# Chunked scan in a hybrid diffusion layer: step weights folded into the exponent, the mask on GpSimd, the sums' loads from ScalarE

## The reference

```python
dt_f = softplus(dt_f + dt_bias_f); dt_b = softplus(dt_b + dt_bias_b)
def ssd_scan(x, dt, a_log, b_in, c_in, init_state):
    A = -exp(a_log)
    xdt = x * dt[..., None]
    a_cs = cumsum((dt * A).reshape(bsz, nc, CHUNK, h), axis=2)
    seg = a_cs[:, :, :, None, :] - a_cs[:, :, None, :, :]
    decay_in = exp(where(lower, seg, -inf))
    scores = einsum('bclhn,bcshn->bclsh', Ch, Bh)
    y_diag = einsum('bclsh,bcshp->bclhp', scores * decay_in, xdt)
    ...
y_f, s_f = ssd_scan(xs, dt_f, a_log_f, bm, cm, init_f)
y_b, s_b = ssd_scan(fl(xs), fl(dt_b), a_log_b, fl(bm), fl(cm), init_b)
y = y_f + fl(y_b) + d_skip[:, None] * xs
```

## Time and profile before

| | |
|---|---|
| median of 3 runs | 2670.51 us (2668.92 to 2671.6) |
| run of the profiled execution | 2666.11 us, span 2664.4 us |
| TensorE busy | 2464.3 us (92%), weight loads 2169.4 us |
| VectorE / ScalarE / GpSimd busy | 2092.3 (79%) / 1095.0 (41%) / 843.7 us (32%) |
| mean granted TensorE clock | 0.968 |

### The profile page before, as it was taken

The page is one execution under the profiler, slowest core; times in us unless marked ns, Lnnn a source line. Parts: engine busy times, 40 slices in busy tenths (PEclk is TensorE's granted clock), DMA queues, the critical chain, the costliest instruction groups (busy, mean ns, idle before and its releaser), DMA issues.

```text
span 2664.4 us, 38495 instructions
## 1 busy us (share of the span) xinstructions
PE 2464.3 (92%) x14858; PEld 2169.4 (81%) x14858; DVE 2092.3 (79%) x3722; ACT 1095.0 (41%) x1785; POOL 843.7 (32%) x621
## 2 busy tenths in 40 slices
PE   6889999999889977997999887999999999999997
PEld 5778888888777767996886786888888888888886
DVE  3767777726667774543999796999999999999999
ACT  4335656534545544314444582333333333233333
POOL 0000000005667660100343583444334434343431
PEclk9999999999999998998999998999999999999998
DMA  7421121235455445332123489999999999999996
GB/s 305 177 105 70 69 99 69 87 133 170 129 182 156 140 140 174 143 135 103 64 71 106 150 243 381 418 417 418 412 419 416 417 408 415 400 415 417 418 409 249
DMA packets 177671, 642.60 MB, mean 241 GB/s; under 512 B 15600, under 2 KB 84304, under 8 KB 117072
## 3 DMA queue, kind: packets, MB, share of 16 engines
q1 hardware_dynamic: 136016, 361.17, 37.7%
q0 software_dynamic: 36864, 268.45, 24.5%
q10 hardware_dynamic: 4608, 10.52, 1.3%
HBM read 580.23 MB, written 59.72 MB: 240 GB/s over the span
## 4 chain that ended last, share of the span: by engine, by line
PE 71%; DVE 16%; DMA 6%; issue 3%; ACT 3%; SPq 1%; DVEq 0%; POOL 0%; PEldq 0%; PEld 0%; ACTq 0%; POOLq 0%
PE c_pp L885 8%; PE p_pa L2606 5%; PE p_pa L2608 5%; PE p_pa L2607 5%; PE p_py L2625 5%; PE p_py L2623 5%; PE p_py L2624 5%; PE o_ps L1718 4%; PE e_ps L2423 4%; PE s_pg L1418 3%; PE p_py L2637 3%; PE g_ps L1093 2%; DMA w_raw<-in_w_stream 2%; PE a_ps L833 2%; DMA s_sums<-sum_rows 2%
## 5 line engine op out<-in xcount | busy, mean ns | idle before, releaser
L2588 POOL DMA_INDIRECT p_uv<-in_uv_rows,merged x256 | 399.8, 1562 | 616.6 <-DVE merged L2761 555.2
L2606 PE MATMUL p_pa<-h2D,w_hi 128*128 128x384 f32 x896 | 318.8, 356 | 19.9 <-DVE w_lo L2715 19.8
L2761 DVE SCALAR_TENSOR_TENSOR merged<-p_uv,p_sw,merged 128x1024 f32<-128x1024 f32 x256 | 328.6, 1284 | 7.1
L2744 DVE CUSTOM_DVE_ANT_0 p_uv<-p_uv,merged 128x1024 f32<-128x1024 f32 x256 | 307.9, 1219 | 10.8 <-DMA p_uv<-in_uv_rows,merged 10.7
L2608 PE MATMUL p_pa<-h2D,w_lo 128*128 128x384 f32 x896 | 303.0, 338 | 0.0
L2607 PE MATMUL p_pa<-h2D,w_hi 128*128 128x384 f32 x896 | 302.9, 338 | 0.0
L2657 ACT ACTIVATE w_hi<-w_raw 128x2048 fp32r<-128x2048 f32 x110 | 210.3, 1912 | 150.5 <-PE p_py L2625 85.6
L2715 DVE TENSOR_TENSOR w_lo<-w_raw,w_hi 128x2048 fp32r<-128x2048 f32 x110 | 251.7, 2288 | 24.9 <-ACT w_hi L2657 24.9
L2623 PE MATMUL p_py<-w_hi,p_wh 128*128 128x512 f32 x672 | 265.4, 395 | 1.2 <-DVE w_lo L2715 1.2
L2625 PE MATMUL p_py<-w_hi,p_wl 128*128 128x512 f32 x672 | 265.3, 395 | 0.0
L2624 PE MATMUL p_py<-w_lo,p_wh 128*128 128x512 f32 x672 | 265.1, 394 | 0.0
(11 more groups left out here) (403 smaller groups left out, 6018.0 us busy)
## 6 DMA issues: line engine op xcount, KB each, us to landing
w_raw<-in_w_stream SPq DMA_DIRECT2D x174, 1024.0 KB
s_sums<-sum_rows SPq DMA_DIRECT2D x40, 512.0 KB, 6.7
g_pairs<-e_st SPq DMA_DIRECT2D x5, 4096.0 KB, 16.9
p_g<-g_pairs SPq DMA_DIRECT2D x64, 320.0 KB
t_ada<-in_w_ada SPq DMA_DIRECT2D x16, 1024.0 KB, 9.5
xc_dram<-c_xc SPq DMA_DIRECT2D x8, 1284.0 KB, 5.4
p_ve<-in_v_early SPq DMA_DIRECT2D x8, 1024.0 KB, 13.1
r_ur<-in_u_early ACTq DMA_DIRECT2D x14, 512.0 KB, 3.7
```

Source lines behind the costliest of these rows:

```text
L2588: nc.gpsimd.indirect_dma_start(uv[:, k % RING, :], None, K.uv_rows, bass.IndirectOffsetOnAxis(K.sidx[:, t, c:c + 1], 0)).then_inc(K.gather ...
L2606: nc.tensor.matmul(ps_a[m][:, :], wh[:, k, cols], K.h2D[0][:, k, :], start=k == 0, stop=False)
L2744: nc.vector.tensor_tensor_reduce(uv[:, b, 0:D], uv[:, b, 0:D], K.hrow[:, t, :], 1.0, 0.0, ALU.mult, ALU.add, sa[:, at:at + 1]).then_inc(do ...
L2761: nc.vector.scalar_tensor_tensor(ys[:, t, :], uv[:, b, D:2 * D], sw[:, at:at + 1], ys[:, t, :], ALU.mult, ALU.add).then_inc(v_done, 1)
```

## The change

The step size goes into the exponent: step size × exp(sum − own sum) becomes exp(sum + (log of the step size − own sum)). `K.minus_sums` becomes `K.offsets`. Both directions get an exponential of their own, and the half that doesn't belong is set to −1e30 in the spread sums before.

- Tokens: VectorE bounds the step size from below (`s2`), ScalarE takes Ln of it and the exponential of minus that, VectorE makes one correction step of the logarithm from it (two instructions) and subtracts the own sums (two). ScalarE's two copies of `minus_sums` go. TensorE's first transposes wait for the decays and for the offsets.
- GpSimd makes `outside` once (0 or −1e30), and in each step adds it to the loaded sums in place (`mask`), one instruction of 128 × 1024 behind `skip` of the step before; it waits for the load. `weights` goes.
- ScalarE takes eight exponentials of 128 columns with a bias column, the forward ones into `M`, the backward ones into `B`. `shift` goes. They wait for `mask`, for `outputs` and for `mix` of two steps before. Then ScalarE waits for its own exponentials and issues the load of the sums of step b + 2. SyncE loads only those of steps 0 and 1.
- VectorE adds `B` to `M` instead of multiplying by the weights. `lesser` goes.

```diff
@@ -356,7 +356,8 @@
     row = sb("q_row", [P, 2 * UC]); b_row = sb("q_brow", [P, 2 * UC])
-    dtA = sb("q_dtA", [P, NT, 64]); sums_row = sb("q_sums", [P, 4 * P])
+    dtA = sb("q_dtA", [P, NT, 64]); logs = ax; logs_done = sem("t_logs"); inv_done = sem("t_inv"); offsets_done = sem("t_offsets")
+    sums_row = sb("q_sums", [P, 4 * P])
@@ -497,11 +498,13 @@
         S.hi(act, 2, 0)
+        act.wait_ge(dtA_done, 1)
+        nc.scalar.activation(logs[:, :, :], s2[:, :, :], ACT.Ln).then_inc(logs_done, 1)
+        act.wait_ge(logs_done, 1)
+        nc.scalar.activation(ex[:, :, :], logs[:, :, :], ACT.Exp, scale=-1.0).then_inc(inv_done, 1)
         act.wait_ge(cum_mm, 2)
...
             nc.scalar.activation(K.decay[:, 3 * j:3 * j + 3, :], ps_cum[j], ACT.Exp).then_inc(cum_exp, 1)
-        for j in range(2):
-            nc.scalar.activation(K.minus_sums[:, j, :], ps_cum[j][:, 0, :], ACT.Copy, scale=-1.0).then_inc(cum_exp, 1)
         for i in range(PAIRS):
@@ -618,10 +621,17 @@
         link(nc.vector.tensor_scalar(nega[:, :], nega[:, :], -1.0, None, ALU.mult))
+        link(nc.vector.tensor_scalar(s2[:, :, :], K.dt[:, :, :], 1.0e-37, None, ALU.max))
         nc.vector.tensor_tensor(dtA[:, :, :], K.dt[:, :, :], nega[:, :].unsqueeze(1).to_broadcast([P, NT, 64]),
...
         S.lo(dve, 2, 0)
+        dve.wait_ge(inv_done, 1)
+        link(nc.vector.tensor_tensor(ex[:, :, :], ex[:, :, :], s2[:, :, :], ALU.mult))
+        link(nc.vector.scalar_tensor_tensor(logs[:, :, :], ex[:, :, :], -1.0, logs[:, :, :], ALU.add, ALU.add))
         dve.wait_ge(cum_exp, 2)
+        for j in range(2):
+            nc.vector.tensor_tensor(K.offsets[:, j, :].rearrange("p (c h) -> p c h", c=NT), logs[:, :, 32 * j:32 * j + 32],
+                                    ps_cum[j][:, 0, :].rearrange("p (c h) -> p c h", c=NT), ALU.subtract).then_inc(offsets_done, 1)
         for r, d in ((1, 0), (4, 1)):
@@ -675,7 +685,8 @@
             else:
-                pe.wait_ge(cum_exp, 4)
+                pe.wait_ge(cum_exp, 2)
+                pe.wait_ge(offsets_done, 2)
             for j in range(4):
@@ -1155,8 +1166,7 @@
     sums = [sb(f"s_sums{i}", [P, 2, HPG, P]) for i in range(2)]
-    X = sb("s_X", [P, HPG, P])
-    W = [sb(f"s_W{i}", [P, HPG, P]) for i in range(2)]; half_W = sb("s_half_W", [P, HPG, P])
+    outside = sb("s_outside", [P, 2, P]); B = [sb(f"s_B{i}", [P, HPG, P]) for i in range(2)]
     M = [sb(f"s_M{i}", [P, HPG, P]) for i in range(2)]
...
@@ -1211,6 +1221,11 @@
         return a, b, f
+    def load_sums(queue, b):
+        g, c = b // NT, b % NT
+        queue.dma_start(sums[b % 2][:, :, :, :].rearrange("p d h l -> p d (h l)"),
+                        K.sum_rows[c, :, 4 * g * P:(4 * g + HPG) * P].partition_broadcast(P)).then_inc(sums_in[b % 2], 16)
@@ -1233,13 +1248,6 @@
-        def load_sums(b):
...
         def store_states(g):
@@ -1262,7 +1270,7 @@
         for b in range(2):
-            load_sums(b)
+            load_sums(sp, b)
         for s in range(2):
@@ -1273,8 +1281,6 @@
                 store_states(q // NT - 1)
-            if NT <= q < NT + STEPS - 2:
-                load_sums(q - NT + 2)
             if q >= 1:
@@ -1320,20 +1326,16 @@
-        def weights(b):
...
-            nc.gpsimd.tensor_tensor(w, w, half_W[:, :, :], ALU.add).then_inc(W_done, 1)
+        def mask(b):
+            rows = sums[b % 2][:, :, :, :]
+            pool.wait_ge(sums_in[b % 2], 16 * (b // 2 + 1))
+            nc.gpsimd.tensor_tensor(rows, rows, outside[:, :, :].unsqueeze(2).to_broadcast([P, 2, HPG, P]), ALU.add).then_inc(masked, 1)
+        for d, tri in enumerate((K.tri_le, K.tri_ge)):
+            nc.gpsimd.tensor_scalar(outside[:, d, :], tri[:, :], 1.0e30, -1.0e30, ALU.mult, ALU.add).then_inc(outside_done, 1)
+        pool.wait_ge(outside_done, 2)
+        mask(0)
         for q in range(SLOTQ):
@@ -1341,10 +1343,10 @@
                     carry(g, 5)
-            if q >= NT - 1 and q - NT + 1 < STEPS:
-                weights(q - NT + 1)
             if b is not None:
                 skip(b)
+                if b + 1 < STEPS:
+                    mask(b + 1)
         K.clear_previous(pool)
@@ -1463,22 +1465,20 @@
-        def shift(b):
+        def exps(b):
             g, c = b // NT, b % NT
-            act.wait_ge(sums_in[b % 2], 16 * (b // 2 + 1))
-            if b:
-                act.wait_ge(E_done, b)
-            for h in range(HPG):
-                at = c * HEADS + 4 * g + h
-                nc.scalar.activation(X[:, h, :], sums[b % 2][:, 0, h, :], ACT.Identity,
-                                     bias=K.minus_sums[:, 0, at:at + 1]).then_inc(shifted, 1)
-        def exps(b):
-            act.wait_ge(least, HPG * (b + 1))
+            act.wait_ge(masked, b + 1)
             if b >= 2:
                 act.wait_ge(y_mm, b - 1)
-            nc.scalar.activation(M[b % 2][:, :, :], X[:, :, :], ACT.Exp).then_inc(E_done, 1)
+                act.wait_ge(EE_done, b - 1)
+            for d, out in enumerate((M[b % 2], B[b % 2])):
+                for h in range(HPG):
+                    at = c * HEADS + 4 * g + h
+                    nc.scalar.activation(out[:, h, :], sums[b % 2][:, d, h, :], ACT.Exp,
+                                         bias=K.offsets[:, d, at:at + 1]).then_inc(E_done, 1)
+            if b + 2 < STEPS:
+                act.wait_ge(E_done, 2 * HPG * (b + 1))
+                load_sums(act, b + 2)
@@ -1514,8 +1514,6 @@
                 exps(b)
-            if q >= NT - 1 and q - NT + 1 < STEPS:
-                shift(q - NT + 1)
             for u, i in todo[:split_point(todo)]:
@@ -1544,22 +1542,11 @@
-        def lesser(b):
...
         def mix(b):
             m = M[b % 2][:, :, :]
-            dve.wait_ge(E_done, b + 1)
-            dve.wait_ge(W_done, b + 1)
-            nc.vector.tensor_tensor(m, m, W[b % 2][:, :, :], ALU.mult).then_inc(WE_done, 1)
-            dve.wait_ge(WE_done, b + 1)
+            dve.wait_ge(E_done, 2 * HPG * (b + 1))
+            nc.vector.tensor_tensor(m, m, B[b % 2][:, :, :], ALU.add).then_inc(EE_done, 1)
+            dve.wait_ge(EE_done, b + 1)
             dve.wait_ge(sc_mm, b + 1)
@@ -1593,8 +1580,6 @@
                 finish(f)
-            if q >= NT - 1 and q - NT + 1 < STEPS:
-                lesser(q - NT + 1)
             if a is not None:
@@ -2898,7 +2883,7 @@
         K.ssq = sb("ssd_ssq", [P, NT, GROUPS])
-        K.dt, K.minus_sums = sb("dt", [P, NT, 64]), sb("minus_sums", [P, 2, NT * HEADS])
+        K.dt, K.offsets = sb("dt", [P, NT, 64]), sb("offsets", [P, 2, NT * HEADS])
         K.decay = sb("decay", [P, 6, NT * HEADS])
...
             K.hT = [h_ctx.enter_context(nc.sbuf_tensor(f"hT{i}", [P, KD, T], F32R)) for i in range(2)]
```

26 lines of the change are left out of this document (2 added, 24 removed).

## The result

The changed kernel takes 2656.22 us (2652.48 to 2656.86, four runs) where the kernel before, timed again beside it, takes 2671.06 (2668.92 to 2671.71, four runs): a ratio of 0.9943, with a 95% interval of 0.9926 to 0.996. That is 14.8 us faster, where 35 had been forecast. The direction and the range hold; the size is not the forecast's but near that of the second rival (2653).

What follows compares the result with a forecast made beforehand. TensorE was taken to bound the kernel, losing time in the scan to waits on ScalarE and VectorE and a lower clock. −11.4 − 11.6 − 5 − 9 + 2 = −35 us gave 2636 us; 8 in 10 range 2618 to 2662.

Steps and rivals of the forecast that it cites:

- the second rival: GpSimd's mask holds VectorE through `finish`; price 17 us, total 2653 us, chance 0.10.
- VectorE's loop (−11.4): `finish`, `lesser`, `weighted` run before TensorE's next `states`; dropping `lesser` shortens ten waits for `s_xs`, −11.4 us.
- So 0.3 us a step: VectorE's cost when GpSimd's mask meets the third and later instructions of `finish`: 0.3 us a step.
- The mask's own length (2.25 us, bounds to 2.56): GpSimd's mask of 1024 elements takes 2.25 us, bounds 1.28 and 2 × 1.28.
- 2.4 us to spare, so nothing for the wait itself: GpSimd's mask ends at about 708.2 us, ScalarE wants it at 710.6, so the wait costs nothing.
- The end of the scan (−5): From 980 us, TensorE's waits for `s_M` shrink without `lesser` ahead of `mix`: 1.2 us in four slots, −5 us.
- The loads (−11.6): Sums loaded two slots ahead, past SyncE's group loads: TensorE's 14.6 us of waits go, 3 put back, −11.6 us.
- the forecast's five: TensorE's five load-loop waits, four for z pieces and the last for a gate piece, together 14.6 us.
- ScalarE (+2): ScalarE's eight exponentials and load issue mostly fit its cover; +2 us for slots with Silu and a weight split.
- The first rival: ScalarE becomes the late one, its later copies costing TensorE; price some 20 us, total 2656, chance 0.12.
- The clock (−9): Stretches of TensorE's lower clock behind waits go with those waits: −9 us, bounds 0 and −16.
- The token phase (0 or +0.7): Once, extra VectorE instructions and ScalarE's Ln and Exp with one or two table loads: 0 or +0.7 us.

Runs made afterwards that it cites:

- b1: The kernel before without `lesser`, so without the backward half of the exponents; 2648.79 us, ratio 0.9925.
- b2: The kernel before with SyncE issuing the load of sums ahead of everything else of its slot; 2649.98 us, ratio 0.9935.
- e2: The changed kernel with the mask on only 16 of the 128 columns, at the same place; 2624.66 us, ratio 0.9835.
- e3: The changed kernel with the loads of sums issued by SyncE again, at their old place behind the group's loads; 2649.53 us, ratio 0.9926.
- e8: e6 with the loads of sums issued by SyncE behind the group's loads, as in e3; 2646.53 us, ratio 0.9912.
- e6: The changed kernel with the mask whole on VectorE, behind `mix` of the step before; 2666.11 us, ratio 0.9988.
- e9: e8 with VectorE's mask moved ahead of `mix`, nothing left out; 2632.31 us, ratio 0.9864.
- e11: e9 with the loads of sums issued by ScalarE again, as in the changed kernel; 2640.33 us, ratio 0.9894.
- e4: The changed kernel with the mask replaced by two fills of the same elements, which read nothing from SBUF; 2633.23 us, ratio 0.9867.

## Why the prediction was right or wrong

**VectorE's loop (−11.4): failed as forecast, and by one term.** That `lesser` lies on the loop and what it is worth was right: b1 shows −11.7. The step that failed is "So 0.3 us a step" for the meeting of mask and `finish`. It measured 1.4 us a step, and the meetings with the mask alone come to 1.1. Two readings led there. I placed the mask from one slot, in which it would end as the third instruction begins. Over the 27 slots from 700 to 960 us it starts between 1.7 us before and 5.2 after TensorE's outputs begin, with a median of 1.4 after; the third instruction starts 2.16 after, and in 23 of the 27 the mask has not ended by then. And I counted one instruction, while all of VectorE's with two SBUF operands can be met: the additions, the product, the weighted rows and `mix`. The row with 3.09 us had been read the earlier trace rows, and the blocking stood in the rival; the median of 0.427 us spoke for the small price, but it is the median of an instruction that met none of the three weight instructions in the whole scan, so it says nothing of what a meeting costs.

**The mask's own length (2.25 us, bounds to 2.56): right,** 2.34 to 2.41 us in 33 of 40 (2.468 mean).

**Its "2.4 us to spare, so nothing for the wait itself": wrong.** The exponentials wait for it 29.9 us. At the end of the scan the two faults feed each other. GpSimd, then ScalarE, then TensorE, in the changed kernel:

```profile
975.11 2.49 DVE L111 TENSOR_TENSOR w_lo<-w_raw,w_hi 128x2048 fp32r<-128x2048 f32 x1
975.41 4.45 POOL L1333 TENSOR_TENSOR s_sums<-s_sums,s_outside 128x1024 f32<-128x1024 f32 x1
979.90 1.28 ACT L1477 ACTIVATE s_M<-s_sums,offsets 128x128 f32<-128x128 f32 x4 [4.72 <-POOL s_sums L1333]
984.30 1.63 PE L1392 MATMUL s_py<-s_xb,s_M 128*128 128x64 f32 x8 [3.23 <-DVE s_M L1551]
```

The low-part split holds the mask, which takes 4.45 us; the exponentials wait 4.72 and TensorE 3.23. The mask itself stands behind `skip`, `skip` behind `squares`, and `squares` behind the exponentials of the same step. I had followed this ring with ScalarE's order of the kernel before.

**The end of the scan (−5): wrong.** The waits for `s_M` are 6.2 us against 6.5, and the wait for the gate copy is 3.57 at 990.03 us where it was 3.19. Over the last 45 us of the scan the two waits were 5.7 and 3.2 before, and are 5.3 and 3.6 in the changed kernel. Without `lesser` alone (b1) they are 1.5 and 7.9, and with the loads first alone (b2) 4.5 and 0.8. So `lesser` did stand ahead of `s_M`, as forecast, but what was gained went into the gate copy, behind ScalarE's waits for the loads. e2 still has 4.4 and 2.4, without `lesser` and with early loads; what makes those is open.

**The loads (−11.6): right in size,** −12.6, with b2 at −12.7 as the check. But these are waits for the z copy alone, of which the forecast's five held 11.4; it had 3.19 more for the gate copy and put back 3. That the lead and not the queue does it was said, and e3 bears it out. The cost of the issue in ScalarE's stream was sized at 0.4 us a step, which is right where ScalarE has cover (0.37 for the issue itself); where it is the late engine it is 0.55 a step, and between e8 and e6 20 us. Between e9 and e11 it is 8, and between e3 and the changed kernel 5 to 7 with overlapping intervals. So +2 was too little for it; by how much in the changed kernel is not settled.

**ScalarE (+2):** an exponential with a bias column is 49.7/156 = 0.32 us, as taken. The first rival did not come: the z waits fell.

**The clock (−9): −5.2 in the changed kernel,** as most of the waits stayed: the four kinds fell by 9.4 us, where 28 had been forecast. In e2 TensorE is busy 354.65 us at 0.98, −13.7, more than the −9.

**The token phase (0 or +0.7): right;** kernels with it start the scan from 602 to 608 us, as those without it do, so it can't be told from nothing.

**The rival** that was given 0.10, with a price of 17 us, was the right mechanism. The changed kernel lies 20 us above e4 by the ratios, whose GpSimd does not read; as the fills are 0.56 us a step shorter, and e4 and e2 differ by 8.6 us for 1.36 us a step, I estimate 3 to 4 of the 20 to be that time and 16 to 17 the blocking. That its total (2653) is near the 2656 measured is partly luck: the whole price of the mask was 29 us against its 17, and the rest of the change gained 9 us more than the forecast. It deserved the larger chance, since the one row about a meeting showed a block of the full length.

## What to carry to other kernels

When work is moved to GpSimd to free VectorE, price the blocking as up to its full SBUF-reading time on VectorE and look for a gap of that length in every step, not in one slot. Here 2.5 us on GpSimd made VectorE's other instructions 1.4 us a step longer, while the same instruction on VectorE is 1.2. Then ask who waits for it: its place in the step was worth 14 us with the engine unchanged, the engine and place together 13 to 16. And for late loads try the order first: one moved call in SyncE's queue gave 17 us without any change of the arithmetic.
